# Second up projection of a feed-forward block: gate and value of a tile as one 2x2 product of quarters by seven products

## The reference, cut to what matters

```python
u2 = _rmsnorm(h, g_ffn_pre[i])
up = _causal_dwconv3(u2 @ w_ffn_up[i], conv_ffn_w[i]) + b_ffn_conv[i]
f_gate, f_val = up[..., :D_FF], up[..., D_FF:]
f = (jax.nn.gelu(f_gate, approximate=True) * f_val) @ w_ffn_down[i]
h = h + _rmsnorm(f, g_ffn_post[i])
```

## Time and profile before

| | us |
|---|---|
| median of 3 runs | 1677.93 |
| lowest and highest | 1677.8, 1679.37 |
| the profiled execution, device time | 1678.03 |
| its span in the profile | 1676.2 |
| PE busy | 1668.7 |
| DVE, ACT, POOL busy | 945.7, 615.7, 969.2 |

### The profile page before, as it was taken

One profiled execution on the slowest core, in us unless ns is written; L12 is line 12 of the kernel. 1 busy time (PEld: TensorE's weight loads), 2 busy tenths in 40 slices (PEclk: granted clock), 3 DMA queues, 4 the chain that ended last, 5 costly groups with the idle time before them and its releaser, 6 DMA issues.

```text
span 1676.2 us, 21936 instructions
## 1 busy us (share of the span) xinstructions
PE 1668.7 (100%) x7770; PEld 1389.9 (83%) x7770; DVE 945.7 (56%) x1652; ACT 615.7 (37%) x1167; POOL 969.2 (58%) x597
## 2 busy tenths in 40 slices
PE   9999999999999999999999999999999999999998
PEld 7888888888888888887888888888888888888887
DVE  7876322156652554166768444438667967775244
ACT  5556311243221222145633322323523137765022
POOL 7555566656666666756756555546664663333654
PEclk9999999999999999999999999999999999999999
DMA  6322222222333332333222222222232221111222
GB/s 212 88 63 89 88 100 100 90 99 88 101 101 100 100 100 100 103 100 113 89 88 75 76 90 99 75 82 88 101 100 73 99 89 51 51 51 64 90 98 77
DMA packets 57335, 152.63 MB, mean 91 GB/s; under 512 B 16928, under 2 KB 17056, under 8 KB 57248
## 3 DMA queue, kind: packets, MB, share of 16 engines
q1 hardware_dynamic: 56240, 149.63, 27.0%
q10 hardware_dynamic: 1008, 1.84, 0.3%
HBM read 149.35 MB, written 2.10 MB: 90 GB/s over the span
## 4 chain that ended last, share of the span: by engine, by line
PE 99%; ACT 0%; DVE 0%; DMA 0%; issue 0%; SPq 0%; ACTq 0%; POOLq 0%; POOL 0%
PE bank L959 29%; PE bank L961 29%; PE bank L960 29%; PE bank L1869 1%; PE bank L1712 1%; PE bank L1709 1%; PE bank L1708 1%; PE bank L1425 1%; PE bank L1426 1%; PE bank L1429 1%; PE bank L1154 1%; PE bank L979 0%; PE bank L1326 0%; PE bank L1322 0%; PE bank L1323 0%; PE bank L1164 0%
## 5 line engine op out<-in xcount | busy, mean ns | idle before, releaser
L863 POOL TENSOR_TENSOR w_lo<-raw,w_hi 128x1024 fp32r<-128x1024 f32 (+2 forms) x275 | 641.5, 2333 | 23.0
L861 POOL TENSOR_SCALAR w_hi<-raw 128x1024 fp32r<-128x1024 f32 (+2 forms) x275 | 285.4, 1038 | 625.0 <-issue 476.8
L959 PE MATMUL bank<-op_hi,w_hi 128*128 128x512 f32 x964 | 378.9, 393 | 0.2 <-DVE r L2741 0.2
L961 PE MATMUL bank<-op_hi,w_lo 128*128 128x512 f32 x964 | 375.9, 390 | 0.0
L960 PE MATMUL bank<-op_lo,w_hi 128*128 128x512 f32 x964 | 375.6, 390 | 0.0
L959 PE MATMUL bank<-r,w_hi 128*128 128x512 f32 x856 | 339.6, 397 | 0.1
L961 PE MATMUL bank<-r,w_lo 128*128 128x512 f32 x856 | 334.2, 390 | 0.0
L960 PE MATMUL bank<-r,w_hi 128*128 128x512 f32 x856 | 333.8, 390 | 0.0
L961 PEld LDWEIGHTS bank<-op_hi,w_lo 128*128 128x128 f32 x964 | 181.0, 188 | 38.1
L959 PEld LDWEIGHTS bank<-op_hi,w_hi 128*128 128x128 f32 x964 | 181.3, 188 | 36.9 <-POOL w_lo L845 0.6
L960 PEld LDWEIGHTS bank<-op_lo,w_hi 128*128 128x128 f32 x964 | 181.3, 188 | 35.8
(11 more groups left out here) (350 smaller groups left out, 2300.8 us busy)
## 6 DMA issues: line engine op xcount, KB each, us to landing
raw<-in_weights SPq DMA_DIRECT2D x267, 512.0 KB, 3.2
out<-h SPq DMA_DIRECT2D x8, 256.0 KB, 2.0
h<-in_x SPq DMA_DIRECT2D x3, 512.0 KB, 8.0
raw<-in_weights SPq DMA_DIRECT2D x8, 128.0 KB, 2.6
raw<-in_weights SPq DMA_DIRECT2D x6, 160.0 KB, 2.5
cst<-in_consts SPq DMA_DIRECT2D x1, 832.0 KB, 11.0
raw<-in_weights SPq DMA_DIRECT2D x3, 256.0 KB, 3.2
rope_cos<-in_p ACTq DMA_DIRECT2D x3, 256.0 KB, 3.6
```

The costliest lines, as they stand in the source:

```text
L861: pool.tensor_scalar(hi, raw[:, r, at:w], 1.0, 0.0, ALU.mult, ALU.add).then_inc(hi_ready, 1)
L863: pool.tensor_tensor(lo, raw[:, r, at:w], hi.bitcast(F32), ALU.subtract).then_inc(split_ready, 1)
L959: pe.matmul(o, ah, bh, start=start, stop=False, skip_group_check=skip)
L961: return pe.matmul(o, al, bh, start=False, stop=stop, skip_group_check=skip)
```

## The change

For a tile of up1, take the weights as a 2x2 matrix of quarters (the two halves of the 1024 inputs by gate and value, each quarter four blocks of 128 x 128) and the tokens as a 2x2 matrix (the two halves of the inputs by the early and the late 256 tokens). The 2x2 product of quarters is made with seven products in place of eight. Each is of 4 blocks and 256 tokens, 12 matmuls, so a tile has 84 matmuls of 256 columns in place of 48 of 512.

- Tokens: the operands are sums of token quarters. They are formed once, in the new stage `norm1` behind `rope` on DVE, that is beside down0: `normal(j)` scales `h` by gain and `rs` for two blocks of inputs, makes the mixed quarters `t1` to `t4`, and with ACT's `normal_high(j)` splits four tiles. The multiplications by `rs` in up1 go.
- Weights: four of the seven operands are quarters as loaded, or in their place, and DVE makes four sums a tile (`seven_sum`), in place in raw or into `fx` and two tables of constants.
- Splits: ACT makes the hi halves (`seven_high`), POOL the lo halves, seven of 128 x 512 a tile, into six half slots.
- Outputs: PE adds in PSUM where two outputs share a product (`both_bank`, `apart_bank`). Between products ACT copies a state of a bank to SBUF (`seven_kept`: `s1`, `s2`, `s5`), and DVE adds it back (`u`, `g`).
- The conv and the gelu of tile i are done during tile i + 1 (`conv_rest`, `value_first`, `gelu`, `gated`).

```diff
+                    pe.wait_ge(norm_d.sem, norm_d.total)
+                    for i in range(HJ):
+                        both, early, late = both_bank(i)[:, EARLY_HALF], apart_bank(i)[:, EARLY_HALF], apart_bank(i)[:, LATE_HALF]
+                        if i >= 4:
+                            pe.wait_ge(d.sem, d.at(f"lo_{i - 4}"))
+                        seven(i, 0, both, start=True)
+                        seven(i, 1, late, start=True)
+                        pe.wait_ge(a.sem, a.at(f"s1_{i}"))
+                        seven(i, 2, both)
+                        seven(i, 3, early)
+                        pe.wait_ge(a.sem, a.at(f"s2_{i}"))
+                        seven(i, 4, both)
+                        pe.wait_ge(a.sem, a.at(f"s5_{i}"))
+                        seven(i, 5, late, stop=True)
+                        pe.wait_ge(d.sem, d.at(f"u_{i}"))
+                        seven(i, 6, both, stop=True)
...
+            for i in range(HJ):
+                for t in range(SEVEN):
+                    n = SEVEN * i + t
+                    hi, lo = seven_flat(n)
+                    pool.wait_ge(part_hi, n + 1)
+                    low = pool.tensor_tensor(lo, seven_source(i, t), hi.bitcast(F32), ALU.subtract)
...
+                def seven_high(n):
...
+                    if n >= 6:
+                        act.wait_ge(*product_done(n - 6))
...
+                    if t in (0, 3, 6):
+                        act.wait_ge(*up1_landed(up1_unit + 2 * i + t // 6))
+                    else:
+                        act.wait_ge(sum_ready, 4 * i + {1: 1, 2: 2, 4: 3, 5: 4}[t])
+                    act.activation(seven_flat(n)[0], seven_source(i, t), ACT.Copy).then_inc(part_hi, 1)
...
+                    for i in range(HJ):
+                        n = SEVEN * i
+                        both = both_bank(i)[:, EARLY_HALF]
+                        seven_kept("s1", i, 0, kept_both(i)[:, EARLY_HALF], both)
+                        seven_high(n + 6)
+                        value_first(i - 1)
+                        seven_high(n + 7)
+                        seven_kept("s2", i, 2, kept_both(i)[:, LATE_HALF], both)
+                        seven_high(n + 8)
+                        gelu(i - 1)
+                        seven_high(n + 9)
+                        seven_kept("s5", i, 3, kept_late(i), apart_bank(i)[:, LATE_HALF])
+                        seven_high(n + 10)
+                        product_high(i - 1)
+                        seven_high(n + 11)
+                        act.wait_ge(d.sem, d.at(f"g_{i}"))
+                        conv_first("g", 0, i)
+                        seven_high(n + 12)
...
+                    if s == 0:
+                        dve.wait_ge(*up1_landed(up1_unit + 2 * i))
+                        dve.wait_ge(*up1_landed(up1_unit + 2 * i + 1))
+                    if s in (1, 3):
+                        dve.wait_ge(sum_ready, 4 * i + (1 if s == 1 else 2))
+                    if i and s != 2:
+                        dve.wait_ge(part_ready, (SEVEN - 1) * (i - 1) + (2, 3, None, 6)[s])
+                    o, x, y = ((fx[:, 3, :], weight_quarter(i, 1, 0), weight_quarter(i, 1, 1)), (const("mla_bias"), fx[:, 3, :], weight_quarter(i, 0, 0)),
+                               (weight_quarter(i, 1, 0), weight_quarter(i, 0, 0), weight_quarter(i, 1, 0)), (const("reset"), weight_quarter(i, 0, 1), const("mla_bias")))[s]
+                    dve.tensor_tensor(o, x, y, ALU.subtract if s else ALU.add).then_inc(sum_ready, 1)
...
                 else:
-                    ffn_block(0, [U0[name] + n + 1 for n in range(2)], 4)
-                    with dve.Fori(0, (HJ - 1) // 2) as i:
-                        for e in range(2):
-                            blk = i * 2 + (1 + e)
-                            ffn_block(blk, [blk * 2 + (U0[name] + n + 1) for n in range(2)], 4 if e else 6)
+                    for i in range(HJ):
+                        seven_sum(i + 1, 0)
+                        conv_rest("g", 0, i - 1)
+                        seven_sum(i + 1, 1)
+                        conv_rest("v", 1, i - 1)
+                        seven_sum(i + 1, 2)
+                        seven_sum(i + 1, 3)
+                        gated(i - 1)
+                        dve.wait_ge(*product_done(SEVEN * i + 4))
+                        sync(a, f"s5_{i}")
+                        add(d, f"u_{i}", both_bank(i)[:, LATE_HALF], both_bank(i)[:, EARLY_HALF], kept_late(i))
+                        gated_low(i - 1)
+                        dve.wait_ge(*product_done(SEVEN * i + 5))
+                        sync(a, f"s2_{i}")
+                        add(d, f"g_{i}", apart_bank(i)[:, :], apart_bank(i)[:, :], kept_both(i))
...
+                        stt(nd, f"x{j}", x[:, :], h[:, j], gcol("g_ffn_pre", j), rs, ALU.mult, ALU.mult)
+                        stt(nd, f"y{j}", y[:, :], h[:, 4 + j], gcol("g_ffn_pre", 4 + j), rs, ALU.mult, ALU.mult)
...
+                    normal(0)
                     split_p(a, d)
+                    for j in range(1, 4):
+                        normal(j)
+                    dve.wait_ge(nd.sem, nd.total)
+                    for n in range(4):
+                        seven_sum(0, n)
+                    dve.wait_ge(d.sem, d.total)
```

More of the change, by code:

```diff
@@ L469, in build @@
         for half in (0, 1):
-            stage(f"up{half}", HJ, ["g0", "ge", "v0", "hi"],
-                  ["g", "g1", "g2", "v", "v1", "v2", "pr", "lo"], [])
+            if half == 0:
+                stage("up0", HJ, ["g0", "ge", "v0", "hi"], ["g", "g1", "g2", "v", "v1", "v2", "pr", "lo"], [])
+                stage("norm1", 1, [f"{x}{j}" for j in range(4) for x in ("third", "first", "second", "mixed")],
+                      [f"{x}{j}" for j in range(4) for x in ("x", "y", "t3", "t1", "t2", "t4", "lthird", "lfirst", "lsecond", "lmixed")], [])
+            else:
+                stage("up1", 1, [f"{x}_{i - back}" for i in range(HJ + 1)
+                                 for x, back in (("s1", 0), ("v0", 1), ("s2", 0), ("ge", 1), ("s5", 0), ("hi", 1), ("g0", 0)) if 0 <= i - back < HJ],
+                      [f"{x}_{i - back}" for i in range(HJ + 1)
+                       for x, back in (("g1", 1), ("g2", 1), ("v1", 1), ("v2", 1), ("pr", 1), ("u", 0), ("lo", 1), ("g", 0)) if 0 <= i - back < HJ], [])
             if half == 0:
@@ L925, in split_rounds @@
                         split(k * RAW + r, r, True)
-            split_rounds((first, rank_round - 1))
+            split_rounds((first, up1_unit // RAW))
+            for u in range(up1_unit // RAW * RAW, up1_unit):
+                pool.wait_ge(landed[u % RAW], 16 * (u // RAW + 1 - missing(u)))
+                split(u, u % RAW, True)
+            for i in range(HJ):
[4 more added lines that the diff above has]
+                    low = pool.tensor_tensor(lo, seven_source(i, t), hi.bitcast(F32), ALU.subtract)
+                    if t < SEVEN - 1:
+                        low.then_inc(part_ready, 1)
+                    else:
+                        low.then_inc(split_ready, 2)
+            pool.sem_inc(hi_ready, 2 * HJ)
+            for u in range(up1_end, -(-up1_end // RAW) * RAW):
+                pool.wait_ge(landed[u % RAW], 16 * (u // RAW + 1 - missing(u)))
+                pool.wait_ge(part_done, (SEVEN - 1) * (HJ - 1) + 4)
+                split(u, u % RAW, False)
+            split_rounds((-(-up1_end // RAW), rank_round - 1))
             for u in range((rank_round - 1) * RAW, (rank_round + 2) * RAW):
@@ L1347, in _, with seven @@
                 if half:
[L1348 to L1355 removed]
+                    def seven(i, t, out, start=False, stop=False):
+                        hi, lo = seven_slot(SEVEN * i + t)
+                        if t < SEVEN - 1:
+                            pe.wait_ge(part_ready, (SEVEN - 1) * i + t + 1)
+                        else:
+                            pe.wait_ge(split_ready, u + 2 * i + 2)
+                        for k in range(4):
+                            x_hi, x_lo = seven_tokens(t, k)
+                            mm = split_mm(out, hi[:, k], lo[:, k], x_hi, x_lo, start and k == 0, stop and k == 3, True)
+                        if t < SEVEN - 1:
+                            mm.then_inc(part_done, 1)
+                        else:
+                            mm.then_inc(unit_done, 2)
+                    norm_d = S["norm1"]["dve"]
+                    pe.wait_ge(norm_d.sem, norm_d.total)
[14 more added lines that the diff above has]
+                        seven(i, 6, both, stop=True)
                 else:
@@ L2258, in _ @@
                 else:
[L2259 to L2262 removed]
+                    for i in range(HJ):
[16 more added lines that the diff above has]
+                        seven_high(n + 12)
+                    value_first(HJ - 1)
+                    gelu(HJ - 1)
+                    product_high(HJ - 1)
                 name = f"down{half}"
@@ L2265, in _, with normal_high @@
                     enter(act, "act", "rope", ())
```

(6 more changed lines are left out.)

154 lines of the change are left out of this document (136 added, 18 removed).

## The result

| | us |
|---|---|
| median of 4 runs of the changed kernel | 1695.42 (1694.19 to 1695.92) |
| median of 4 runs of the kernel before | 1677.87 (1677.8 to 1679.37) |
| ratio | 1.0101, interval 1.0084 to 1.0119 |
| span of the profiled execution | 1693.7 (before 1676.2) |
| up1, from its first matmul to the next stage's | 535.89 to 664.76 (before 529.31 to 648.99) |

A forecast was written before the change was run, and what follows sets the result against it. TensorE was taken to bound the kernel, busy 1668.7 of 1676.2 us. 7.4 (start) + 2.5 + 3.0 (first two tiles) + 8 x 0.4 - 0.5 = 15.6 us on 1678 gave 1694 us, range 1682 to 1706.

The forecast's parts named there:

- tile 10: Last tile of up1: no sums left to make, 0.5 us less.
- TensorE's own part: Each up1 tile: 84 matmuls at 0.123 us, 10.3 us against 10.88, winning 6.0 us in all.
- The port that POOL and DVE share: In up1 tiles, SBUF-only sums and POOL's lows take turns: each sum adds 0.55 us to POOL, whose tile takes 11.0.
- DVE's tile in the steady state: Tiles 2 to 9: DVE's work and waits set 11.3 us a tile, 0.4 more than before.
- The start of the stage: Before up1: TensorE waits for mixed tokens and the first low half, starting at 536.7, not 529.31: +7.4 us.
- Tile 0: First up1 tile: waits for the second product's part and the half add make it 13.4 us, +2.5.
- Tile 1: Second up1 tile: DVE waits for tile 2's weights with other work queued behind; 13.9 us, +3.0.
- The clock: After the pause before up1: half-speed matmuls might add 1 us, giving 1695 us, in the forecast's upper part.
- Faster: Rival for up1: the lock hits seldom and TensorE's 10.3 us sets the tile; 1673 us, chance 0.09.
- No change: Rival for up1: start loses 3, first tiles 2, others run at 10.4; +0.7, 1679 us, chance 0.10.

The follow-up runs named there:

- bank_operand: Changed kernel with one input of each weight sum read from a PSUM bank (output wrong) and three pairs of banks, not four: 1678.86 us.
- early_mix: Changed kernel with norm1 made during the first half of down0, ahead of the last rope steps: 1685.08 us, ratio to before 1.0044.
- conv_before_sum: Changed kernel with, in tile 1 alone, DVE making tile 0's gate convolution ahead of sum 0 of tile 2: 1691.84 us.
- changed_again: The changed kernel run once more without an edit: 1693.35 us.
- same_no_copies: copies_moved without the copies to banks and with four pairs of banks, so all sums read SBUF twice: 1678.53 us.
- copies_moved: Changed kernel with early norms, three bank pairs, fourth sum last, tile 1's convolution and gelu table earlier, two quarters a tile copied to banks in ACT's idle time: 1671.35 us.
- three_pairs: Changed kernel with banks in a rotation of three pairs in place of four, sums as they were: 1694.32 us.
- table_early: Changed kernel with the gelu's table loaded on ACT ahead of tile 0, not in tile 1: 1696.89 us.

## Why the prediction was right

It came within 1.4 us of the median. The sum was 15.6 us and the difference of the medians is 17.5. Of the 1.9 us between them, 1.6 are the fall of the clock in ple1, which no term had; tile 1 (1.25 more) against the start and tile 10 (0.8 and 0.3 less) nearly cancel, which is luck. The steps:

- **TensorE's own part** (0.123 us a matmul, 10.3 us a tile). It is 0.120 and 10.08, the tile 0.2 us cheaper, which tile 10 and the steady tiles of bank_operand show.
- **The port that POOL and DVE share.** Right: bank_operand shows the mechanism with every sum in place. The sizes were off in both directions. A sum costs POOL less than the 0.55 that I took: its lows average 1.48 us (112.7 us by 76), 0.19 over the free 1.29, 1.3 us a tile and not 2.2. POOL's tile is then 7 x 1.48 less overlaps, about 10.2, and not 11.0. DVE pays more: four sums at 1.50 are 3.2 us over the free price, where I had 2.7. The Trainium skill (SBUF — State Buffer, "SBUF: two separate sides") has DVE take the pair of ports only in certain modes or with two SBUF inputs against a GpSimd instruction that reads SBUF; bank_operand agrees, 0.68 us a sum and 1.30 us a low once one input is in PSUM. A full block at every sum would have cost POOL 4 x 0.69 = 2.8 us a tile; it lost 1.3.
- **DVE's tile in the steady state** (11.3 us). Measured 11.28, and 11.19 without the slow clock in tile 2. The bound is DVE, as said: it is busy for 21.6 of the 22.4 us of tiles 4 and 5. That the number is so close is partly luck: DVE's waits were 0.5 us more than I said, and its instructions overlap by some 0.08 us at each of the up to 12 handovers of a tile, at most 1.0 us, which I hadn't taken off. I didn't foresee the pairs of 10.5 and 11.9.
- **The start of the stage** (+7.4). Measured +6.6; `norm1` ended at 534.63 and not at 535.5 (the waits that I had listed add up to 535.3), with the first low behind it at 535.75 and not 536.6. early_mix shows that nothing else makes the pause.
- **Tile 0** (+2.5). Measured +2.5, in other pieces. Over a full product's 1.44 us the first took 1.5 more (the wait for the second part, 1.3 in the forecast), the last had 0.6 us to wait for the half add (1.5 in the forecast), and the second, fourth and fifth took 0.6, 0.3 and 0.3 more. 2.2 us of it went with early_mix.
- **Tile 1** (+3.0, measured +4.25): the term that was mis-sized, though its end was not. Forecast were a start at 550.1 and an end at 564.0; measured were 549.32 and 564.45. The end hangs on tile 2's weights: sum 0 of tile 2 started at 552.78 and `u_1` was done at 562.6 (562.5 in the forecast). Those weights were asked for at 547.0 and 547.6 (548.5 in the forecast) and the second unit landed at 552.7, 5.1 us after its issue and 5.7 after the first, where I took 5. So the 0.8 us that the stage was ahead was lost again in tile 1, and the last product took 1.78 us and not 1.44, at a lower clock at its end. That `u_1` is the end of a list behind the weights, conv_before_sum shows: one convolution less behind the wait, and it was done at 561.5. In early_mix tile 1 began 9.1 us sooner and ended 8.2 us sooner, 9.1 without its slower last product; the weights are asked for after tile 0's last low, so they move with POOL's list, and the wait stays.
- **The clock.** The granted clock fell to 0.50, that is TensorE at 1.2 GHz, at 533.2 us, inside the pause, and stayed there up to 540.0 us (the window of the pause has a mean of 0.81, the one behind it 0.50); the first matmuls came every 0.213 us. The forecast had +1 in its upper part for it, and the wait for the second part hid nearly all. The Trainium skill (TensorE: Matmul & The Clock Gate, "HAM oscillation") says that an idle gap puts the clock back to half, and here the trace agrees: the clock fell while TensorE did nothing for 7.1 us, and early_mix, without the pause, has no fall there. The two further falls, at 564 and 779 us, cost 0.9 and 1.6 us against changed_again, and weren't in the forecast at all.

That the rivals didn't come true has one reason each. *Faster* needed sums that find POOL idle: of the 44 only some did. *No change* needed a start that loses 3 us and steady tiles of 10.4. The time of the second is reached by same_no_copies, that of the first by copies_moved, each after the causes named here were taken away.

## What to carry to other kernels

Before helpers are loaded with work for a shorter TensorE, list for each new DVE instruction whether both inputs are in SBUF while POOL works there; here this doubled its price, and one input in a bank gave it back. A product less saved 0.8 us a tile and everything else was the price of feeding it, so the gain came only when mixing, sums and copies all lay in time that was idle anyway. A copy must stand in its engine's list where the engine waits, not where it is first possible: the same two copies, one instruction earlier in ACT's order, were worth 0.7 us a tile.

## What the hardware showed

- The granted clock fell to 0.50 not only in the pause of 7.1 us. In the changed kernel it also fell at the end of tile 1 (563.9 to 567.3 us), in which TensorE had stopped for 1.6 and 3.1 us. early_mix, three_pairs and table_early had such a fall too. changed_again, with the same stops, had none, nor had conv_before_sum (stops of 1.1 and 2.4 us).
- It fell in ple1 in two of the thirteen profiles (the changed kernel and table_early) with TensorE busy for the whole window, ahead of it two runs of eight matmuls of one column, at 776.0 and 777.8 us in the changed kernel, where the clock fell at 778.9. In three_pairs the same instructions came 0.3 us later at the full clock. What decides is open; no run here separates it.
- At the full clock a matmul of 256 columns cost 0.120 us (10.08 by 84) and one of 512 cost 0.227, so half the columns cost 53% of the time.
